# Two scans of a delta rule on one core: half-step order against level-by-level order, and decays off the PE

## The chip, the cores and the metric

One core of a Trainium2 chip runs the whole program. The metric is device time in microseconds (us) of one execution, the median of several runs. Engines are named as in the profile: PE is TensorE's matmul, PEld its weight loads, DVE is VectorE, ACT is ScalarE, POOL is GpSimd, SP is SyncE, whose queue issues DMAs.

## The reference, cut to what matters

The kernel is one layer of a model: a mixer with three branches and a mixture of experts. The change lies in one branch, the gated delta rule, which is scanned in chunks of 128 tokens, forward and backward, with 4 heads of width 128. Context and latent tokens together are 18 chunks, so each direction makes 18 steps.

```python
gc = jnp.cumsum(chunks(g), axis=-1)
diff = gc[..., :, None] - gc[..., None, :]
decay = jnp.where(tri, jnp.exp(jnp.where(tri, diff, 0.0)), 0.0)
m = jnp.where(strict, jnp.einsum('nbhik,nbhjk->nbhij', kb, kc) * decay, 0.0)
a_mat = m + jnp.eye(CHUNK, dtype=f32)
sol = lax.linalg.triangular_solve(a_mat, rhs, left_side=True, lower=True, unit_diagonal=True)
qk = jnp.where(tri, jnp.einsum('nbhik,nbhjk->nbhij', qc, kc) * decay, 0.0)

def step(s, inp):
    qg_i, kg_i, u_i, w_i, qk_i, gl_i = inp
    v_new = u_i - jnp.einsum('bhck,bhkv->bhcv', w_i, s)
    o = jnp.einsum('bhck,bhkv->bhcv', qg_i, s) + jnp.einsum('bhij,bhjv->bhiv', qk_i, v_new)
    s = s * gl_i[..., None, None] + jnp.einsum('bhck,bhcv->bhkv', kg_i, v_new)
    return s, o
```

Per chunk and direction the kernel builds the matrix from the key products and the decays, inverts it (1 + m) in levels of doubling block size, and uses the inverse with the carried state.

## The kernel before, in words

The program runs its stages one after the other with a barrier between them: projections and convolution, the mixer's other branches, `delta_rule` (line 1302), `merge`, the output projection, the choice of experts and the experts. Only `delta_rule` and three lines of the stage ahead of it are touched.

`delta_rule` holds both directions d = 0 and 1. A *half* (lines 1510, 1655, 1778) is one chunk of one direction: its inverse runs through levels 1 to 6. A level is a group of TensorE products `first` (line 1553, 128x64 per head, written at line 1545), a copy of its result to SBUF by ScalarE (`partial`, line 1477), a second group `second` (line 1564, 128x96 per head, line 1575), and VectorE's `update` (line 1726): a predicated copy into `um` and, up to level 4, a transposition of `um` into `tm`. At level 6 TensorE turns `um` itself (`turn_u`, line 1578) and ScalarE copies it to `tm` (`turned`, line 1483). Every link waits for the one before it. Level 1 starts from `mn`, which ScalarE copies after TensorE has turned the matrix `mt` (`turn_m`, line 1650; `matrix`, line 1471).

In the gaps of this chain the half carries other work, in an order written out by hand. From the half before it, the *old* one (the other direction): `values`, `from_state`, `from_chunk` and `state` (lines 1583 to 1614). For the *new* one that comes next (the other direction again): `keys`, `scores`, `known`, `turn_m` on TensorE (lines 1623 to 1653), the decays, and VectorE's `matrix`, `begin`, `rest` (lines 1736 to 1759). Some groups are split by heads to fit: three heads of `keys` in one gap, the fourth in the next. `halves` (line 1355) walks the halves (0, n), (1, n) through 18 steps; the middle 16 steps are a loop with two steps in its body.

The decays of a chunk come from TensorE: VectorE's `gate` (line 1717) multiplies a triangle of ones by the gates' high and low parts (`gth`, `gtl`), two products of 512 columns (`exponents`, line 1616, its matmuls are lines 1620 and 1621) sum them in PSUM, and ScalarE takes the exponential (line 1463). GpSimd multiplies the triangle by beta (`sb`, line 1435). The decays that scale the keys and queries by row are exponentials written to DRAM in the stage ahead (`eg_d`) and loaded for each chunk by SyncE, broadcast over the partitions, with the four tensors of the chunk.

Each direction has four PSUM banks of its own, A to D. A serves `first`, `known` and `state`; B serves `keys`, `turn_m` and `turn_u`; C serves `second`, `scores` and the output; D serves `exponents` and `values`. GpSimd's queue (`head`, line 1431) makes `ke`, `qg`, `kg`, `qk` and renews `um`. SyncE loads a chunk two steps ahead once the state has been updated (line 1404).

## Time and profile before

| what | us |
|---|---|
| median of 3 runs | 4169.45 (4168.18 to 4175.18) |
| the profiled execution | 4168.63 |
| its span | 4167.1 |
| granted clock over the span | 0.979 of full |
| PE busy over the span | 3970.8 (95%) |

A busy time is the time in which at least one instruction of the engine runs. A group of instructions stands with its count and the mean of one; "idle before" is the time its engine waited just before it, with what released it. Times of a timeline are microseconds from the start of the span. A matmul of float32 operands appears as two records, each with its own weight load, so a group over four heads has eight loads; a transposition has one per head.

### The profile page before, as it was taken

To read this page: it belongs to the slowest core of one execution; us is meant where nothing else is said; L and a number is where in the kernel's file an instruction comes from. 1 tells how busy PE (TensorE), PEld (TensorE's weight loads), DVE (VectorE), ACT (ScalarE), POOL (GpSimd) and SP (SyncE) were. 2 spreads that over 40 slices of the span, in tenths; PEclk is the share of its full clock that TensorE was granted. 3 is DMA by queue.
4 is the path that set the end of the run, shared out by engine and by line. 5 is a ranking of instruction groups with operands and counts; after the bars stand their busy time and mean duration, and the time that the engine had idled before them with its cause. 6 is when DMAs were issued, how large, how long until landed. Compare 5 with 4: busy or idle time off the path is not lost. (4 is left out here: it accounts for less than half of the span.)

```text
span 4167.1 us, 57860 instructions
## 1 busy us (share of the span) xinstructions
PE 3970.8 (95%) x20112; PEld 3065.1 (74%) x20112; DVE 2292.2 (55%) x3037; ACT 1531.4 (37%) x2482; POOL 791.7 (19%) x698
## 2 busy tenths in 40 slices
PE   8999999999989999999999999989589999999998
PEld 3444446456769999998778787878478888888887
DVE  4665500356646666665444534344467776777675
ACT  5333411226632222223333424222144444444443
POOL 2999100011113333332000000000100000000000
PEclk9999999999999999999999999999699999999999
DMA  7445341021132222221534444244257676767773
GB/s 289 125 134 140 93 127 39 11 65 33 25 140 65 79 82 78 76 76 41 200 101 169 144 127 152 88 138 152 110 177 215 209 219 206 220 207 217 211 218 101
DMA packets 240185, 551.99 MB, mean 132 GB/s; under 512 B 38316, under 2 KB 99276, under 8 KB 237516
## 3 DMA queue, kind: packets, MB, share of 16 engines
q1 hardware_dynamic: 207964, 435.45, 33.0%
q0 software_dynamic: 32112, 115.11, 9.4%
q8 instruction: 67, 1.10, 0.1%
q14 instruction: 42, 0.34, 0.0%
HBM read 440.44 MB, written 99.68 MB: 130 GB/s over the span
## 5 line engine op out<-in xcount | busy, mean ns | idle before, releaser
L2767 DVE TENSOR_TENSOR sb_we_low<-sb_we,sb_we_high 128x1024 fp32r<-128x1024 f32 x377 | 458.3, 1222 | 121.6 <-ACT sb_we_high L2717 121.6
L2717 ACT ACTIVATE sb_we_high<-sb_we 128x1024 fp32r<-128x1024 f32 x377 | 392.2, 1048 | 142.3 <-PE ey L2681 142.3
L329 PE MATMUL p_ps<-sb_hT,sb_ring 128*128 128x512 f32 (+1 forms) x960 | 373.4, 550 | 1.8 <-ACT sb_raw L462 1.8
L2121 DVE TENSOR_TENSOR sb_wm_low<-sb_wm,sb_wm_high 128x1024 fp32r<-128x1024 f32 x127 | 155.3, 1223 | 399.4 <-ACT sb_wm_high L2034 399.4
L2666 PE MATMUL eg<-sb_xe_parts,sb_we_high 128*128 128x512 f32 x1024 | 373.3, 398 | 1.6 <-DVE sb_xe_parts L2762 1.6
L2666 PE MATMUL eu<-sb_xe_parts,sb_we_high 128*128 128x512 f32 x1024 | 371.9, 396 | 0.0
L329 PEld LDWEIGHTS p_ps<-sb_hT,sb_ring 128*128 128x128 f32 x960 | 181.8, 190 | 188.4 <-issue 180.9
L1976 PE MATMUL pg<-sb_hb_high,sb_wm_high 128*128 128x512 f32 x768 | 304.5, 396 | 9.4 <-DVEq L2093 5.3
L1977 PE MATMUL pg<-sb_hb_low,sb_wm_high 128*128 128x512 f32 x768 | 301.0, 392 | 0.0
L1978 PE MATMUL pg<-sb_hb_high,sb_wm_low 128*128 128x512 f32 x768 | 300.8, 392 | 0.0
L2665 PE MATMUL eg<-sb_xe_parts,sb_we_low 128*128 128x256 f32 x896 | 251.3, 280 | 0.0
L2665 PE MATMUL eu<-sb_xe_parts,sb_we_low 128*128 128x256 f32 x896 | 251.2, 280 | 0.0
L851 PE MATMUL mix_ps<-sb_hT,sb_ring 128*128 128x512 f32 (+1 forms) x544 | 231.7, 583 | 2.7 <-ACTq L1037 2.7
L2625 POOL DMA_INDIRECT out<-sb_ybe,sb_ti x32 | 51.0, 1593 | 889.0 <-DVE sb_ybe L2802 830.5
L2666 PEld LDWEIGHTS eg<-sb_xe_parts,sb_we_high 128*128 128x128 f32 x1024 | 192.5, 188 | 37.0 <-issue 1.8
L2666 PEld LDWEIGHTS eu<-sb_xe_parts,sb_we_high 128*128 128x128 f32 x1024 | 192.4, 188 | 34.5
L2060 ACT ACTIVATE sb_sg<-pg 128x512 f32<-128x512 f32 x96 | 57.1, 595 | 411.3 <-PE pg L1978 411.3
L851 PEld LDWEIGHTS mix_ps<-sb_hT,sb_ring 128*128 128x128 f32 x544 | 103.7, 191 | 126.0 <-issue 125.1
L1976 PEld LDWEIGHTS pg<-sb_hb_high,sb_wm_high 128*128 128x128 f32 x768 | 145.7, 190 | 42.4 <-DVEq L2092 5.5
L2775 DVE TENSOR_REDUCE sb_sue<-eu 128x256 f32<-128x512 f32 x128 | 88.5, 691 | 153.8 <-PE eu L2666 153.8
L2665 PEld LDWEIGHTS eu<-sb_xe_parts,sb_we_low 128*128 128x128 f32 x896 | 168.2, 188 | 6.1
L2665 PEld LDWEIGHTS eg<-sb_xe_parts,sb_we_low 128*128 128x128 f32 x896 | 168.2, 188 | 6.0
(433 smaller groups left out, 8469.0 us busy)
## 6 DMA issues: line engine op xcount, KB each, us to landing
sb_we<-in_w_ex SPq DMA_DIRECT2D x384, 512.0 KB, 4.5
sb_wm<-in_w_gates SPq DMA_DIRECT2D x96, 512.0 KB, 3.6
sb_wrow<-in_w_mod_row POOLq DMA_DIRECT2D x64, 256.0 KB, 3.7
sb_wm<-in_w_br SPq DMA_DIRECT2D x32, 512.0 KB
sb_ring<-in_w_ch POOLq DMA_DIRECT2D x19, 512.0 KB, 4.7
sb_eg<-eg_d SPq DMA_DIRECT2D x36, 256.0 KB, 3.8
sb_lk<-k_d SPq DMA_DIRECT2D x36, 256.0 KB, 4.3
sb_lq<-q_d SPq DMA_DIRECT2D x36, 256.0 KB, 4.6
```

The source lines that it names most:

```text
L329: last = nc.tensor.matmul(ps[:, b % BANKS, 0:wd], w[:, kind, k], g.hT[:, k, t0:t0 + wd], start=(k == 0), stop=(k == KD - 1))
L851: last = nc.tensor.matmul(ps[:, b, 0:wd], w[:, (n + ZF) % 3, k], g.hT[:, k, t0:t0 + wd], start=(k == 0), stop=(k == KD - 1))
L1976: nc.tensor.matmul(bank[:], high, rh[:, k], start=(k == ks[0]), stop=False)
L1977: nc.tensor.matmul(bank[:], high, rl[:, k], start=False, stop=False)
L1978: last = nc.tensor.matmul(bank[:], low, rh[:, k], start=False, stop=(k == ks[-1]))
L2060: a(sg[:, br], pg[br][:], ACT.Sigmoid).then_inc(s.sig, 1)
L2121: v.tensor_tensor(wl[n], w[n], wh[n], ALU.subtract).then_inc(s.wl, 1)
L2665: nc.tensor.matmul(bank[:, 0:CAP], low, xh[:, u, k], start=False, stop=False)
L2666: last = nc.tensor.matmul(bank[:], high, both, start=(k == 0), stop=(k == KD - 1))
L2717: nc.scalar.activation(wh[:, n % CUT], w[:, n % RAW], ACT.Copy).then_inc(s.wh, 1)
L2767: v.tensor_tensor(wl[:, n % CUT], w[:, n % RAW], wh[:, n % CUT], ALU.subtract).then_inc(s.wl, 1)
L2775: v.tensor_reduce(su[:, f % 2], pu[f % 2][:].rearrange("p (a t) -> p t a", a=2), AX_X, ALU.add).then_inc(s.usum, 1)
```

## The change

Both directions of a step now go through the levels together. On every engine a level is direction 0 and then direction 1, and between such pairs stand whole groups of other work: the last step's values, outputs and state, and the next step's set-up. `walk` takes the place of `halves`. The new order of each engine follows (lines of the new code, `both(n, lev)` being the level's copy or update for d = 0, then 1):

```python
def walk(eng, step):
    for n in range(2):
        step(n, n, n > 0, True)
    with eng.Fori(1, STEPS // 2 - 1) as i:
        for u in range(2):
            step(2 * i + u, u, True, True)
    for n in range(STEPS - 2, STEPS):
        step(n, n % 2, True, n < STEPS - 1)
...
# SyncE
def step(n, u, old, new):
    for d in range(2):
        if old:
            store(d, n - 1, place(nc.sync, d, n - 1), 1 - u)
        if not isinstance(n, int) or n < STEPS - 2:
            ahead = place(nc.sync, d, n + 2)
            sem = (s[d].ld0, s[d].ld1)[u]
            sp.wait_ge(s[d].qg, n + 1)
            first_loads(d, ahead, u)
            sp.wait_ge(s[d].kg, n + 1)
            sp.dma_start(lkt[d][u][:], g.kt_d[ahead]).then_inc(sem, 16)
            sp.wait_ge(s[d].r, n + 1)
            sp.dma_start(lvt[d][u][:], g.vt_d[ahead]).then_inc(sem, 16)
...
# GpSimd
def scale(d, n, u):
    q = s[d]
    at = place(nc.gpsimd, d, n)
    pool.wait_ge(q.eg, n + 1)
    wait(pool, q.ks, n)
    tt(ke[d][:], lk[d][u][:], gr[d][u][:], ALU.mult).then_inc(q.ke, 1)
    wait(pool, q.sup, n - 1)
    hold(pool, q.held)
    copy(el[d][u][:], gr[d][u][:, :, last_token(d):last_token(d) + 1]).then_inc(q.el, 1)
    wait(pool, q.op, n)
    tt(qg[d][:], lq[d][u][:], gr[d][u][:], ALU.mult).then_inc(q.qg, 1)
    wait(pool, q.su, n)
    tt(kg[d][:], lkt[d][u][:], col(g.esb, d, at), ALU.mult).then_inc(q.kg, 1)
def scores(d, n, u):
    q = s[d]
    pool.wait_ge(q.qkr, n + 1)
    pool.wait_ge(q.dq, n + 1)
    tt(qk[d][u][:], qr[d][:], dq[d][:], ALU.mult).then_inc(q.qkv, 1)
def step(n, u, old, new):
    for d in range(2):
        if old:
            renew(d, n - 1, 1 - u)
        scale(d, n, u)
        if new:
            scores(d, n + 1, 1 - u)
...
# ScalarE
def row_decays(d, n, u):
    act.wait_ge(s[d].df, n + 1)
    a(gr[d][u][:], gr[d][u][:], ACT.Exp).then_inc(s[d].eg, 1)
def step(n, u, old, new):
    v = 1 - u
    both(n, 1)
    if old:
        values(0, n - 1, v)
    both(n, 2)
    if old:
        output(0, n - 1, v)
    if new:
        row_decays(0, n + 1, v)
        exponent(0, n + 1, v)
    both(n, 3)
    if old:
        values(1, n - 1, v)
    both(n, 4)
    if new:
        raw_scores(0, n + 1, v)
        matrix(0, n + 1, v)
    both(n, 5)
    if old:
        output(1, n - 1, v)
    if new:
        row_decays(1, n + 1, v)
        exponent(1, n + 1, v)
    for d in range(2):
        partial(d, n, 6)
        turned(d, n, u)
    if new:
        raw_scores(1, n + 1, v)
        matrix(1, n + 1, v)
    if isinstance(n, int) and n >= STEPS - 2:
        for i in range(2):
            split_high(2 * (n - STEPS + 2) + i)
...
# TensorE
def turn_u(d, n, u):
    q = s[d]
    pe.wait_ge(q.vu, NL * n + NL - 1)
    if d == 0:
        wait(pe, s[1].vn, n)
    else:
        pe.wait_ge(s[0].t5e, n + 1)
    turn(b_val, um[d][u]).then_inc(q.t5, 1)
def values(d, n, u):
    q = s[d]
    pe.wait_ge(q.vu, NL * n + NL)
    pe.wait_ge(q.r, n + 1)
    pe.wait_ge(s[1].t5e if d == 0 else s[0].vn, n + 1)
    each(b_val, um[d][u], rb[d]).then_inc(q.vp, 1)
def state(d, n, u):
    q = s[d]
    pe.wait_ge(q.kg, n + 1)
    wait(pe, s[1 - d].r, n + 1 + d)
    each(b_state, kg[d], vn[d]).then_inc(q.su, 1)
def known(d, n, u):
    q = s[d]
    pe.wait_ge(q.ke, n + 1)
    pe.wait_ge(q.z, 1)
    wait(pe, q.sup, n)
    wait(pe, s[1 - d].r, n + d)
    each(b_state, ke[d], st[d]).then_inc(q.ks, 1)
def step(n, u, old, new):
    v = 1 - u
    def firsts_of(lev):
        for d in range(2):
            first(d, n, u, lev)
    def seconds_of(lev):
        for d in range(2):
            second(d, n, u, lev)
    firsts_of(1)
    if old:
        values(0, n - 1, v)
    seconds_of(1)
    if old:
        from_state(0, n - 1, v)
    firsts_of(2)
    if old:
        from_chunk(0, n - 1, v)
    seconds_of(2)
    if old:
        state(0, n - 1, v)
    if new:
        keys(0, n + 1, v, (0, 1))
    firsts_of(3)
    if new:
        keys(0, n + 1, v, (2, 3))
    if old:
        values(1, n - 1, v)
    seconds_of(3)
    known(0, n, u)
    firsts_of(4)
    if new:
        scores(0, n + 1, v)
    seconds_of(4)
    if new:
        turn_m(0, n + 1, v)
    if old:
        if new:
            pe.wait_ge(s[0].qkr, n + 2)
        from_state(1, n - 1, v)
    firsts_of(5)
    if old:
        from_chunk(1, n - 1, v)
    seconds_of(5)
    if old:
        state(1, n - 1, v)
    if new:
        keys(1, n + 1, v, (0, 1))
    for d in range(2):
        first(d, n, u, 6)
        turn_u(d, n, u)
    if new:
        keys(1, n + 1, v, (2, 3))
    known(1, n, u)
    seconds_of(6)
    if new:
        scores(1, n + 1, v)
        turn_m(1, n + 1, v)
...
# VectorE
def difference(d, n, u):
    at = place(nc.vector, d, n)
    loaded(dve, d, n, u)
    wait(dve, s[d].dq, n)
    v.tensor_tensor(dec[d][:], gr[d][u][:], col(g.gsums, d, at), ALU.subtract).then_inc(s[d].df, 1)
def clamp(d, n, u):
    dve.wait_ge(s[d].df, n + 1)
    dve.wait_ge(s[d].bar, 1)
    v.tensor_tensor(dec[d][:], dec[d][:], heads(bar[:, d]), ALU.min).then_inc(s[d].cl, 1)
def step(n, u, old, new):
    w = 1 - u
    def both(lev):
        for d in range(2):
            update(d, n, u, lev)
    both(1)
    if new:
        difference(0, n + 1, w)
        clamp(0, n + 1, w)
    both(2)
    if old:
        state(0, n - 1, w)
    both(3)
    if new:
        matrix(0, n + 1, w)
    rest(0, n, u)
    both(4)
    if new:
        begin(0, n + 1, w)
        difference(1, n + 1, w)
        clamp(1, n + 1, w)
    both(5)
    if old:
        state(1, n - 1, w)
    if new:
        matrix(1, n + 1, w)
        begin(1, n + 1, w)
    both(6)
    rest(1, n, u)
    if isinstance(n, int) and n >= STEPS - 2:
        for i in range(2):
            split_low(2 * (n - STEPS + 2) + i)
```

The decays leave TensorE. The stage ahead stores the cumulated gates (`gc_d`) and not their exponentials. SyncE loads them broadcast into `gr`; VectorE subtracts the column of the chunk and takes the minimum with a table `bar` that is 0 in the triangle and -1e30 outside; ScalarE takes the exponential of `dec` in place and, apart from it, of `gr` in place. `gate`, `exponents` and GpSimd's `sb` product are gone; VectorE multiplies by beta's column itself. GpSimd has a small copy more per chunk (`el`, 128x4, the last token's decays). `mn`, `tm` and `qk` have two buffers per direction. The eight PSUM banks are dealt out anew: one `first` and one `second` bank for each direction, and four shared by both (`b_val`, `b_out`, `b_key`, `b_state`), with waits of one direction for the other where they change hands. SyncE's loads two steps ahead are split: cumulated gates, keys and queries once `qg` is made, `lkt` once `kg` is, `lvt` once `rest` is.

```diff
-                        if (n, b) == (NZ, 2):
-                            act.wait_ge(sd.own, 27)
-                            a(g.gdh, gdf, ACT.Copy).then_inc(sd.gh, 1)
...
-                                for j, to in enumerate((g.egc[:, d], g.esb[:, d])):
-                                    a(to, pdec[:, 2 * d + j].rearrange("p (n h) -> p n h", h=H), ACT.Exp).then_inc(sd.ex, 1)
+                                for j, (to, func) in enumerate(((g.gsums[:, d], ACT.Copy), (g.esb[:, d], ACT.Exp))):
+                                    a(to, pdec[:, 2 * d + j].rearrange("p (n h) -> p n h", h=H), func).then_inc(sd.ex, 1)
...
+        lq, lk, lkt, lvt, gr, um, ob, mn, tm, qk = map(four, ("lq", "lk", "lkt", "lvt", "gr", "um", "ob", "mn", "tm", "qk"))
+        el = four("el", 1)
-        bank = [[psum(nc, c, f"dr{d}{b}", (P, H, P)) for b in "abcd"] for d in range(2)]
+        firsts, seconds = ([psum(nc, c, f"dr_{n}{d}", (P, H, P)) for d in range(2)] for n in ("first", "second"))
+        b_val, b_out, b_key, b_state = (psum(nc, c, f"dr_{n}", (P, H, P)) for n in ("val", "out", "key", "state"))
...
-                    act.wait_ge(q.mat, n + 1)
-                    wait(act, q.dq, n)
-                    a(dec[d][:], D_[:], ACT.Exp).then_inc(q.exp, 1)
+                    act.wait_ge(s[d].cl, n + 1)
+                    a(dec[d][:], dec[d][:], ACT.Exp).then_inc(s[d].exp, 1)
...
-                def exponents(d, n, u):
-                    q, (A, B, C_, D_) = s[d], bank[d]
-                    pe.wait_ge(q.gt, 2 * n + 2)
-                    wait(pe, q.vn, n)
-                    mm(flat(D_), after[:, d], flat(gh[d]), start=True, stop=False)
-                    mm(flat(D_), after[:, d], flat(gl[d]), start=False, stop=True).then_inc(q.mat, 1)
...
-                    v.tensor_tensor(dq[d][:], dec[d][:], sb[d][:], ALU.mult).then_inc(q.dq, 1)
+                    v.tensor_tensor(dq[d][:], dec[d][:], col(g.beta, d, at), ALU.mult).then_inc(q.dq, 1)
...
-        g.beta, g.egc, g.esb, g.gdl = (sbuf(nc, c, n, [P, 2, POS, H])[:] for n in ("beta", "egc", "esb", "gdl"))
-        g.gdh = sbuf(nc, c, "gdh", [P, 2, POS, H], F32R)[:]
+        g.beta, g.gsums, g.esb = (sbuf(nc, c, n, [P, 2, POS, H])[:] for n in ("beta", "gsums", "esb"))
```

## Rows read from the trace of the kernel before

**Rows 1.** Busy by stretch: us, then busy us and count of each engine, PEclk, DMA.
```profile
1230.48:1250.80 20.32, 17.00 (x106) 15.29 (x107) 9.23 (x14) 3.55 (x8) 7.43 (x6) 0.83 0.61 228
1499.80:1520.21 20.41, 19.92 (x162) 18.55 (x163) 12.53 (x21) 5.88 (x12) 6.86 (x6) 1.00 0.26 68
1255.00:1935.00 680.00, 662.83 (x5371) 618.38 (x5369) 419.64 (x700) 196.87 (x402) 227.70 (x200) 1.00 0.24 75
```

**Rows 2.** Timeline, where halves start (level 1) and the last values.
```profile
1230.48 1.10 PE L1545 MATMUL dr0a<-sb_um,sb_mn 128*128 128x64 f32 x8 [0.69 <-ACT sb_mn L1475]
...
1253.58 1.08 PE L1545 MATMUL dr1a<-sb_um,sb_mn 128*128 128x64 f32 x8
...
1273.86 1.08 PE L1545 MATMUL dr0a<-sb_um,sb_mn 128*128 128x64 f32 x8
...
1930.63 1.08 PE L1545 MATMUL dr0a<-sb_um,sb_mn 128*128 128x64 f32 x8
...
1971.65 1.16 PE L1545 MATMUL dr1d<-sb_rb,sb_um 128*128 128x128 f32 x8 [0.65 <-DVE sb_um L1730]
```

**Rows 3.** Timeline of one half of direction 1, levels 1 to 5.
```profile
1502.63 0.74 DVE L1730 COPY_PREDICATED sb_um<-sb_consts_sb,dr1c 128x256 f32<-128x256 uint32 x1 [2.35 <-PE dr1c L1575]
...
1503.42 0.97 PEld L1545 LDWEIGHTS dr1a<-sb_um,sb_mn 128*128 128x128 f32 x8 [0.44 <-DVE sb_um L1730]
...
1504.31 0.53 PEld L1596 LDWEIGHTS dr0c<-sb_qg,sb_st 128*128 128x128 f32 x4
...
1504.57 0.38 ACT L1481 ACTIVATE sb_pm<-dr1a 128x256 f32<-128x256 f32 x1 [1.20 <-PE dr1a L1545]
...
1505.00 0.97 PEld L1575 LDWEIGHTS dr1c<-sb_pm,sb_tm 128*128 128x128 f32 x8
...
1505.89 0.75 PEld L1604 LDWEIGHTS dr0c<-sb_qk,sb_vn 128*128 128x128 f32 x6
...
1506.41 0.43 DVE L1730 COPY_PREDICATED sb_um<-sb_consts_sb,dr1c 128x256 f32<-128x256 uint32 x1 [1.35 <-PE dr1c L1575]
...
1506.89 0.97 PEld L1545 LDWEIGHTS dr1a<-sb_um,sb_mn 128*128 128x128 f32 x8 [0.25 <-DVE sb_um L1730]
...
1509.58 0.19 PEld L1620 LDWEIGHTS dr0d<-sb_gth,sb_after 128*128 128x128 f32 x1
...
1510.24 0.97 PEld L1545 LDWEIGHTS dr1a<-sb_um,sb_mn 128*128 128x128 f32 x8 [0.36 <-DVE sb_um L1730]
...
1514.21 1.08 DVE L1766 SCALAR_TENSOR_TENSOR sb_st<-sb_st,sb_eg,dr0a 128x128 f32<-128x128 f32 x4
```

**Rows 4.** By form, 1215 to 1975 us: count | busy us, mean ns of one.
```profile
L1734 DVE STREAM_TRANSPOSE sb_tm<-sb_um 128x512 f32<-128x512 f32 x144 | 102.4, 711 | 5.0
...
L1730 DVE COPY_PREDICATED sb_um<-sb_consts_sb,dr1c 128x256 f32<-128x256 uint32 x108 | 52.6, 487 | 124.0 <-PE dr1c L1575 124.0
...
L1751 DVE COPY_PREDICATED sb_um<-sb_consts_sb,sb_mt 128x512 f32<-128x512 uint32 x36 | 34.1, 947 | 0.3 <-DVE sb_mt L1744 0.2
...
L1741 DVE TENSOR_TENSOR sb_dq<-sb_dec,sb_sb 128x512 f32<-128x512 f32 x36 | 24.9, 692 | 4.0 <-POOL sb_sb L1435 2.2
...
L1499 ACT ACTIVATE sb_ob<-dr0c 128x512 f32<-128x512 f32 x18 | 10.8, 597 | 35.1 <-PE dr0c L1604 35.1
```

**Rows 5.** Line 1720, the gates: duration ns min/median/max.
```profile
L1720 DVE TENSOR_TENSOR sb_gth<-sb_consts_sb,sb_gdh x36: 1010/1019/1515, 1216.1 to 1934.9; 128x512 fp32r<-128x512 f32 x36
L1720 DVE TENSOR_TENSOR sb_gtl<-sb_consts_sb,sb_gdl x36: 651/1350/1360, 1217.1 to 1938.2; 128x512 fp32r<-128x512 f32 x36
```

**Rows 6.** Line 1438, GpSimd: duration ns min/median/max.
```profile
L1438 POOL TENSOR_TENSOR sb_ke<-sb_lk,sb_eg x36: 1265/1713/1722, 1224.3 to 1935.3; 128x512 f32<-128x512 f32 x36
```

**Rows 7.** DMAs of one step (1500 to 1541 us): count, KB, us to landing.
```profile
sb_lvt<-vt_d SPq DMA_DIRECT2D x2, 256.0 KB, 5.5
```

**Rows 8.** Timeline of the start of the stage and of its end.
```profile
1224.28 1.78 PEld L1545 LDWEIGHTS dr0b<-sb_lk 128*128 128x128 f32 x8 [5.44 <-DMA sb_lvt<-vt_d]
...
1974.70 0.60 ACT L1499 ACTIVATE sb_ob<-dr1c 128x512 f32<-128x512 f32 x1 [1.25 <-PE dr1c L1604]
```

More of the change, by code:

```diff
@@ L1539, in _ @@
+                walk(nc.scalar, step)
+                for d in range(2):
+                    values(d, STEPS - 1, 1)
+                    output(d, STEPS - 1, 1)
             @block.tensor
@@ L1655, in half @@
-                def half(cur, old, new):
-                    d, n, u = cur
-                    first(d, n, u, 1)
+                    turn(b_key, mt[d]).then_inc(q.t0, 1)
+                def step(n, u, old, new):
+                    v = 1 - u
+                    def firsts_of(lev):
+                        for d in range(2):
+                            first(d, n, u, lev)
+                    def seconds_of(lev):
+                        for d in range(2):
+                            second(d, n, u, lev)
+                    firsts_of(1)
@@ L1686, in half @@
[L1686 removed]
+                        keys(1, n + 1, v, (0, 1))
+                    for d in range(2):
+                        first(d, n, u, 6)
+                        turn_u(d, n, u)
                     if new:
[L1688 to L1689 removed]
+                        keys(1, n + 1, v, (2, 3))
+                    known(1, n, u)
+                    seconds_of(6)
                     if new:
[L1691 removed]
@@ L1692, in half @@
-                    turn_u(d, n, u)
-                    first(d, n, u, 6)
-                    if new:
-                        turn_m(*new)
-                        known(*new, (2, 3))
-                    second(d, n, u, 6)
-                every = range(H)
-                for d in range(2):
-                    pe.wait_ge(s[d].aft, 1)
-                exponents(0, 0, 0)
-                keys(0, 0, 0, every)
-                known(0, 0, 0, every)
-                scores(0, 0, 0, every)
-                turn_m(0, 0, 0)
@@ L1707, in _ @@
-                halves(nc.tensor, half)
-                end = (1, STEPS - 1, 1)
-                values(*end, every)
-                from_state(*end, every)
-                from_chunk(*end, every)
+                        scores(1, n + 1, v)
+                        turn_m(1, n + 1, v)
+                for d in range(2):
+                    keys(d, 0, 0)
+                    scores(d, 0, 0)
+                    turn_m(d, 0, 0)
+                walk(nc.tensor, step)
+                for d in range(2):
+                    if d == 1:
+                        pe.wait_ge(s[0].oe, STEPS)
+                    values(d, STEPS - 1, 1)
+                    from_state(d, STEPS - 1, 1)
+                    from_chunk(d, STEPS - 1, 1)
@@ L1792, in half @@
-                    update(d, n, u, 5)
+                        state(1, n - 1, w)
                     if new:
-                        begin(*new)
-                        rest(*new)
-                    update(d, n, u, 6)
-                    if turn_of(d, n) is not None:
-                        split_low(turn_of(d, n))
-                for d in range(2):
-                    v.tensor_copy(after[:, d], g.dirt(d, 1)).then_inc(s[d].aft, 1)
-                for part in range(2):
-                    gate(part, 0, 0, 0)
@@ L1803, in _ @@
-                matrix(0, 0, 0)
-                begin(0, 0, 0)
-                rest(0, 0, 0)
-                halves(nc.vector, half)
+                        matrix(1, n + 1, w)
[3 more added lines that the diff above has]
+                    if isinstance(n, int) and n >= STEPS - 2:
+                        for i in range(2):
+                            split_low(2 * (n - STEPS + 2) + i)
+                for d in range(2):
+                    v.tensor_scalar(bar[:, d], g.dirt(d, 0), -1.0, -NEG, ALU.add, ALU.mult).then_inc(s[d].bar, 1)
@@ L1809, in late_data @@
+                for d in range(2):
+                    difference(d, 0, 0)
+                    clamp(d, 0, 0)
+                    matrix(d, 0, 0)
+                    begin(d, 0, 0)
+                walk(nc.vector, step)
 def late_data(t, lev):
```

322 lines of the change are left out of this document (125 added, 197 removed).

## Prediction

> **What bounds the kernel now.** I first look for the stage in the page, then at the busy times by stretch. In the delta rule VectorE works 62% of the time, ScalarE 29%, GpSimd 33%, and PE 97%, at the full clock [rows 1]. A busy time counts pipelined tails, though, so I go to where halves start: 1273.86 for step 1 and 1930.63 for step 17, hence 656.8 us for 16 steps, **41.05 us a step**, 20.5 a half [rows 2]. Then the timeline of one half. A group of eight records starts a slot of its own every 0.89 us: `second` at 1505.00, the next group at 1505.89; `first` at 1503.42, the next at 1504.31 [rows 3]. That is **0.111 us for each weight load**, whatever the width (64, 96 or 128 columns). A half has 160 such loads: 96 of the levels, 56 of seven groups of other work, 8 of two transpositions. That makes 17.8 us. The rest, 2.7 us of a half, is the two `exponents` products (from 1509.58, before the next group at 1510.24, part of which is a wait) and gaps: the level's chain is longer than the work laid into it, as at 1506.89, where PE had waited for VectorE since 1506.56 (1505.89 plus six loads) [rows 3]. So PE's instruction stream is the floor, and a latency chain that is a little too long lies on top of it.
>
> **The chain's lengths.** From the start of `first` to where `second` may start: 1503.42 to 1504.95, when the copy ends, plus 0.05: 1.6 us, of which 0.89 is `first` itself. From the start of `second` to where the next `first` may start: 1505.00 to 1506.89, 1.9 us; 2.1 at level 1, whose predicated copy takes 0.74 instead of 0.43 [rows 3].
>
> **PE in the new order.** A step has 2 × 160 = 320 loads, 35.6 us. I wrote the slots out one after the other from the start of a step (t = 0), 0.89 for a group of four heads and 0.45 for a transposition or two heads, and asked of each group whether what it waits for is there. `first` of d = 0 runs from 0, of d = 1 from 0.89, `values` from 1.78, `second` from 2.67 and 3.56, `from_state` 4.45, level 2 from 5.34, and so on: level 3 from 11.13, level 4 from 16.92, level 5 from 22.7, level 6 from 28.5, the last `turn_m` from 35.2.
> - first to second: the other direction's `first` (0.89) already covers the missing 0.7. No gap in any level.
> - second to first, d = 0: the other `second` and one group, 1.78, cover the missing 1.0 (1.2 at level 1).
> - second to first, d = 1: VectorE is the link. Its copy for d = 1 stands behind copy and transposition of d = 0 (0.49 and 0.71 [rows 4]). At level 1: 3.95 to 4.69, 5.44, then 5.48 to 6.22; `first` is due at 6.23. That is a gap of 0.05. At levels 2 to 4 there is 1 us to spare.
> - VectorE's work between: `difference` and `clamp` of d = 0 from 7.0 to 8.4, before level 2's copy at 9.3; `state` (1.08 [rows 3]) 11.8 to 12.9; `matrix` and `rest` 18.0 to 20.2, before 20.9; `begin` (0.95 + 0.71 [rows 4]), `difference` and `clamp` of d = 1 from 23.3 to 26.7, after which level 5's copy, ready at 26.7, ends at 27.2 for a `first` due at 28.5.
> - step to step: `scores` of d = 1 end at 35.4, ScalarE copies them until 36.05 and only then `mn` until 36.7 (0.60 each [rows 4]). `first` of d = 1 is due 0.89 after the step's start at 35.6, that is 36.5: a gap of 0.2.
>
> **What is removed.** The `exponents` leave PE (about 0.45 us a half once their wait is taken off, 0.66 with it), `gate` leaves VectorE (1.0 and 1.35 us a half [rows 5]), the `sb` product GpSimd. **What is added.** `difference` and `clamp` on VectorE. No row shows them; the nearest of the same kind and size is the product at 0.69 [rows 4], the gates at 1.35 are the upper end [rows 5]. I take 0.7, as they meet GpSimd in few places, and keep 1.35 for the range. A second exponential on ScalarE, 0.60 each, at 8.9 and 26.3, where ScalarE is idle; without that cover it would cost 1.2 a step. A 128x4 copy on GpSimd, between nothing and the 0.6 of ScalarE's 512 columns, in idle time either way. The split loads: direction 0's last is issued at about 20.7 and lands 5.5 later [rows 7]; `difference` wants it at 42.6. Direction 1's is issued at 36.6 and wanted at 60. SyncE's queue waits longer for each, but its stores have two buffers, so nothing is late.
>
> **Two engines at one port.** The gates took 0.65 us once and 1.35 in the median [rows 5], and GpSimd's product 1.27 at least and 1.71 in the median [rows 6]: operations with two inputs in SBUF stretch each other when the two engines' meet. In the new order `begin` and `clamp` of d = 1 meet GpSimd's `ke` and `qg`. With the 0.7 that rows 5 show on top of each, the two end at 28.1 instead of 26.7 and level 5's copy at 28.6, a gap of 0.1, which I add. The Trainium skill (SBUF — State Buffer, "SBUF: two separate sides") says more: a VectorE operation with two SBUF inputs and a GpSimd operation exclude each other, and the later one waits for the whole of the other. Rows 5 and 6 neither refuse that nor need it. The rival that it gives is the second below.
>
> **The sum.** A step: 35.6 + 0.05 + 0.2 + 0.1 = 35.95. The loop's turn and odds: the averaged half is 0.11 over the one of rows 1, so 0.2 a step, kept. **36.2 us**.
> - Steps 1 to 16: 16 × (41.05 − 36.2) = −77.6.
> - Step 0: 43.4 before [rows 2], with a clock of 0.83 in its first half [rows 1]. Now 256 loads (no old work), 28.5, with gaps of 0.7 at two levels without filling and 4.3 for the slow clock: 33.5, −9.9. The old first half took 23.1 for 128 loads [rows 2], 2.6 more than a full one, though it had 3.6 us less to do; its chain's gaps are the rest.
> - Step 17: 41.0 before. Now 280 loads, 31.2, and 1.3 because four of ScalarE's copies for the next stage (0.60 each by rows 4, 2.4, of which `first` and `values` cover 1.1) stand ahead of its first level: −8.5.
> - Start: the first load is there at 1224.28 [rows 8], the first level began 6.2 later [rows 2]. Now both directions must be set up: `difference` 0.7, `clamp` 0.7, exponential 0.65, two products 1.45, `begin` 1.75, then for d = 1 0.7 + 0.7 + 0.65 + 1.45 + 0.7 for `turn_m`: 9.5. +3.3.
> - End: 1971.65 to 1975.30 before, one direction's values and output [rows 2, 8]. Now two, of which the second waits for the first's output in the shared bank: 7.5. +3.9.
> - The stage ahead (one copy and one subtraction of 160 columns fewer): 0.
>
> Sum −88.8 against the profiled 4168.63 (its span is 4167.1): 4079.8. The median of the runs is 0.8 above the profiled one: **4081 us**.
>
> **The rivals.**
> 1. *The gaps return in part.* 90 us rest on every group being ready on time in a stream without slack of its own. One late group moves all behind it. For it: level 1 has no slack and level 5 1.3 us, and 12 cross-direction waits on shared banks are new. Against it: all other slacks are above 0.7. If half of the old gaps stay, 38.1 a step: 17 × 1.9 = 32 more, 4113.
> 2. *Exclusion at the port decides.* If `begin` and `clamp` of d = 1 each wait for a whole product of GpSimd (1.27 [rows 6]), level 5's copy ends at 29.7, a gap of 1.2 where the sum has 0.1: 16 × 1.1 = 18 more, 4099. Rows 5 and 6 show the stretching; against it stands that the gates are gone, so that there are fewer meetings in all. It is what the skill's rule would do here.
> 3. *Slower: VectorE's queue order takes over.* In every level d = 1's copy stands behind d = 0's copy and transposition, and set-up stands ahead of the next level. It decides once each of the six levels loses 0.93 us (5.6 a step, 4.85 of it to break even, the rest for start and end). If each level loses one further copy and transposition (1.2), a step is 43.4 and the kernel about 4215. Against it: VectorE has some 24 us of work in 36, and the slots above leave it 1 us at most levels.
> 4. *The new order brings nothing, only the products' departure does*: the chain of a level stays what PE waits for, 2 × 0.6 a step: 4145.
>
> **The numbers.** Forecast 0.60 (own range 4072 to 4094), rivals 1 and 2 together 0.29, rival 4 0.05, rival 3 0.04, and 0.02 for no difference. A measurement can tell 0.2%, 8 us. The range runs from 4070 (no gap at all, 35.6 a step, less a us or two at the start) to 4122 (rival 1 with the upper price of the new operations). Faster 0.93, same 0.03, slower 0.04.
>
> **What would show it.** Right: `first` of step 17 about 579 us after step 1's; PE's gaps within a step under 1 us; nothing on lines of the products with `after`; the first level of the stage at about 1234. `difference` near 0.7 for d = 0 and above for d = 1. Wrong: PE's weight loads waiting for VectorE's `um` in several levels (rivals 1 and 3), VectorE busy over 27 us a step or its two-input operations at 1.3 (rival 2), or slots longer than 0.111, which would move everything.

## Result and the profile after

The changed kernel took **4075.68 us** (median of 4 runs, 4068.34 to 4079.47) against 4169.1 for the kernel before beside it (4 runs, 4168.18 to 4175.18): ratio **0.9771, interval 0.9754 to 0.9788**. The forecast was 4081, range 4070 to 4122. The profiled execution is the slowest of the four, 4079.47 with a span of 4077.9, so sums below are made against 4079.47 − 4168.63 = −89.2.

First the stage by stretches (columns: us, then busy us and count of PE, PEld, DVE, ACT, POOL, then PEclk, DMA share, GB/s): the first 20 us after both directions' set-up, one whole step, and steps 1 to 16 with their edges. They answer to [rows 1].

```profile
1235.00:1255.00 20.00, 20.00 (x124) 20.00 (x122) 9.91 (x17) 4.42 (x10) 4.84 (x5) 0.66 0.58 215
1522.20:1558.00 35.80, 35.80 (x323) 35.72 (x321) 22.74 (x43) 12.53 (x27) 12.04 (x12) 1.00 0.27 88
1255.00:1845.00 590.00, 588.78 (x5262) 587.23 (x5262) 375.74 (x692) 207.12 (x430) 197.68 (x197) 1.00 0.27 84
```

A step has some 320 weight loads in 35.80 us, and PE is busy for all of it. In 590 us PE stands still for 1.2. VectorE's share is 22.74 us of a step, 64%.

Then PE's timeline, at the places that carry the sum (start and length in us, engine, line, operation, tiles, count; in brackets the idle time ahead and what ended it). They answer to [rows 2] and [rows 8]; lines 1583, 1612 and 1588 of this kernel are the plain products, `second` and the transpositions.

```profile
1225.09 2.07 PE L1583 MATMUL dr_key<-sb_lk 128*128 128x128 f32 x8 [13.30 <-DMA sb_lvt<-vt_d]
...
1234.68 0.66 PE L1588 MATMUL dr_key<-sb_consts_sb,sb_mt 128*128 128x128 f32 x4 [2.56 <-DVE sb_mt L1788]
1235.17 3.32 PE L1583 MATMUL dr_first<-sb_um,sb_mn 128*128 128x64 f32 x16
1238.29 3.67 PE L1612 MATMUL dr_second<-sb_pm,sb_tm 128*128 128x96 f32 x16
...
1264.47 1.10 PE L1583 MATMUL dr_first<-sb_um,sb_mn 128*128 128x64 f32 x8 [1.22 <-DVE sb_um L1774]
...
1271.72 2.01 PE L1583 MATMUL dr_first<-sb_um,sb_mn 128*128 128x64 f32 x16
...
1844.63 2.01 PE L1583 MATMUL dr_first<-sb_um,sb_mn 128*128 128x64 f32 x16
...
1876.55 1.08 PE L1583 MATMUL dr_val<-sb_rb,sb_um 128*128 128x128 f32 x8
...
1880.16 1.16 PE L1583 MATMUL dr_val<-sb_rb,sb_um 128*128 128x128 f32 x8 [0.69 <-ACT sb_ob L1517]
...
1883.20 0.60 ACT L1517 ACTIVATE sb_ob<-dr_out 128x512 f32<-128x512 f32 x1 [1.25 <-PE dr_out L1642]
```

Step 1 starts at 1271.72 and step 17 at 1844.63: 572.9 us for 16 steps, **35.81 a step** where it was 41.05. The weight-load stream inside a step shows why there is next to nothing left to gain from order. From start to start, a group of 8 loads takes 0.89 us and one of 16 takes 1.79, one behind the other; only the first group of a step takes 1.90:

```profile
1522.26 1.98 PEld L1583 LDWEIGHTS dr_first<-sb_um,sb_mn 128*128 128x128 f32 x16
1524.16 0.97 PEld L1583 LDWEIGHTS dr_val<-sb_rb,sb_um 128*128 128x128 f32 x8
1525.05 1.87 PEld L1612 LDWEIGHTS dr_second<-sb_pm,sb_tm 128*128 128x128 f32 x16
1526.84 0.97 PEld L1635 LDWEIGHTS dr_out<-sb_qg,sb_st 128*128 128x128 f32 x8
1527.73 1.87 PEld L1583 LDWEIGHTS dr_first<-sb_um,sb_mn 128*128 128x128 f32 x16
```

Last, groups by form over the whole stage (after the count: busy us and mean ns, then the idle time ahead and its releaser): the new operations and PE's largest groups.

```profile
L1583 PE MATMUL dr_first<-sb_um,sb_mn 128*128 128x64 f32 x1728 | 211.9, 274 | 1.2 <-DVE sb_um L1774 1.2
L1774 DVE COPY_PREDICATED sb_um<-sb_consts_sb,dr_second 128x256 f32<-128x256 uint32 x216 | 102.7, 476 | 188.3 <-PE dr_second L1612 188.0
L1765 DVE TENSOR_TENSOR sb_dec<-sb_dec,sb_bar 128x512 f32<-128x512 f32 x36 | 26.6, 739 | 1.2
L1759 DVE TENSOR_TENSOR sb_dec<-sb_gr,sb_gsums 128x512 f32<-128x512 f32 x36 | 23.8, 660 | 8.0 <-DMA sb_lvt<-vt_d 8.0
L1450 POOL TENSOR_TENSOR sb_qg<-sb_lq,sb_gr 128x512 f32<-128x512 f32 x36 | 53.6, 1488 | 86.9 <-PE dr_out L1642 86.9
L1448 POOL COPY sb_el<-sb_gr 128x4 f32<-128x4 f32 x36 | 14.4, 399 | 0.0
```

`first` waits for VectorE's `um` 1.2 us in the whole stage, while VectorE waits 188 us for PE: the roles are those of a kernel bound by PE's stream.

### The profile page after: what moved, and what is told of

It is laid out like the page before. It is cut to its first block and busy times, and to the rows that moved or that the text cites. A ratio compares the mean times of both kernels' runs of the same rounds, so it can differ in the third digit from the quotient of the medians.

```text
span 4077.9 us, 57895 instructions
## 1 busy us (share of the span) xinstructions
PE 3900.2 (96%) x20032; PEld 3041.6 (75%) x20032; DVE 2249.7 (55%) x3032; ACT 1545.3 (38%) x2517; POOL 764.3 (19%) x697
## 3 DMA queue, kind: packets, MB, share of 16 engines
q1 hardware_dynamic: 207964, 435.45, 33.5%
## 5 line engine op out<-in xcount | busy, mean ns | idle before, releaser
L1583 PE MATMUL dr_first<-sb_um,sb_mn 128*128 128x64 f32 x1728 | 211.9, 274 | 1.2 <-DVE sb_um L1774 1.2
L1612 PE MATMUL dr_second<-sb_pm,sb_tm 128*128 128x96 f32 x1728 | 211.4, 276 | 0.3 <-ACT sb_pm L1499 0.3
L1583 PEld LDWEIGHTS dr_first<-sb_um,sb_mn 128*128 128x128 f32 x1728 | 207.3, 194 | 2.0 <-DVE sb_um L1774 1.4
L1774 DVE COPY_PREDICATED sb_um<-sb_consts_sb,dr_second 128x256 f32<-128x256 uint32 x216 | 102.7, 476 | 188.3 <-PE dr_second L1612 188.0
L1612 PEld LDWEIGHTS dr_second<-sb_pm,sb_tm 128*128 128x128 f32 x1728 | 205.0, 195 | 0.5 <-ACT sb_pm L1499 0.5
```

Source lines behind the costliest of these rows:

```text
L1583: last = mm(out[:, h], lhs[:, h], rhs[:, h], start=True, stop=True)
L1612: last = mm(wide(seconds[d])[:, h], tm[d][u][:, h], pm[d][:, h * HALF:h * HALF + WIDE], start=True, stop=True)
```

## The experiments

The theory: the old order left PE waiting for each level's chain (PE, ScalarE, PE, VectorE), and joining the directions level by level fills these waits until only 320 loads of 0.111 us are left. The rivals: that the departure of the `exponents` products and the gates brought the gain, or that a shorter VectorE did. Ratios are to the kernel before, measured beside it. "Step" is the mean of steps 1 to 16, taken between starts of the same group 16 steps apart. "Stage" is the delta rule's own time: from the end of PE's last product of the stage ahead to the end of the last output copy. It is taken from there because the stage ahead ended anywhere from 1208.2 to 1211.9 us, and at 1211.8 and 1209.4 in two profiled executions of the changed kernel itself, so that the bare end of the delta rule carries up to 3.7 us that are not its own. Step and stage come from one profiled execution of each kernel; the kernel before has 41.05 and 764.3, the changed kernel 35.81 and 672.0.

| kernel | median us (range) | ratio [interval] | step us | stage us |
|---|---|---|---|---|
| decays alone, old order | 4175.06 (4170.04–4178.16) | 1.0003 [0.9993, 1.0013] | 40.95 | 772.0 |
| new, without chunk's part | 4064.39 (4060.34–4068.68) | 0.9739 [0.9723, 0.9755] | 34.02 | 636.9 |
| old, without chunk's part | 4180.29 (4174.35–4187.14) | 1.0019 [1.0009, 1.0028] | 41.43 | 779.0 |
| new, clamp twice | 4080.71 (4077.83–4082.30) | 0.9776 [0.9760, 0.9792] | 35.81 | 677.5 |
| new, 8 more loads a step | 4086.83 (4083.39–4093.17) | 0.9794 [0.9778, 0.9811] | 36.70 | 687.9 |
| new, warm start | 4074.09 (4069.55–4076.28) | 0.9761 [0.9745, 0.9777] | 35.81 | 669.4 |
| new, split loads | 4068.74 (4066.76–4070.41) | 0.9752 [0.9736, 0.9769] | 35.81 | 664.3 |
| new, both | 4068.02 (4066.61–4073.64) | 0.9752 [0.9736, 0.9768] | 35.81 | 666.3 |
| new again | 4078.78 (4067.68–4081.54) | 0.9768 [0.9755, 0.9781] | 35.81 | 672.0 |
| split loads again | 4067.11 (4066.18–4074.49) | 0.9752 [0.9738, 0.9765] | 35.81 | 664.3 |
| split, short warm-up | 4079.90 (4075.03–4085.19) | 0.9776 [0.9763, 0.9789] | 35.81 | 666.3 |
| the same, end in free banks | 4079.01 (4076.11–4081.67) | 0.9772 [0.9758, 0.9785] | 35.81 | 663.1 |

The kernel before took 4173.55 beside rows 1 to 4 of the table, 4171.85 beside rows 5 to 8 and 4173.24 beside rows 9 to 12. The ratio of the changed kernel was 0.9771.

**The decays alone.** The old order, with the products and gates gone:

```diff
-                    mm(flat(D_), after[:, d], flat(gh[d]), start=True, stop=False)
-                    mm(flat(D_), after[:, d], flat(gl[d]), start=False, stop=True).then_inc(q.mat, 1)
...
-                    a(dec[d][:], D_[:], ACT.Exp).then_inc(q.exp, 1)
+                    act.wait_ge(s[d].cl, n + 1)
+                    a(dec[d][:], dec[d][:], ACT.Exp).then_inc(s[d].exp, 1)
```

> The order of the kernel before (half by half), with only the decays moved: no gates, no products of the decays on the PE, no beta product on GpSimd; VectorE subtracts and clamps, ScalarE has a second exponential. Theory A (the gain of the change is the order: in the old order the PE waits at the ends of the levels' chain, and the group behind the products waited for VectorE's um until 1510.19 anyway): 4150 to 4169 us, no more than 20 us of the 93. Rival B (the gain is the work taken off the PE and VectorE, 0.66 and some 1.0 us a half): 24 us or more, 4145 or below.

The time did not move, so that not even a part of the 20 us allowed for came, and a step went from 41.05 to 40.95. Two views of this kernel say why: the windows (1260 to 1830; the second row is the kernel before), and PE's groups by line in the same stretch.

```profile
1260.00:1830.00 570.00, 546.55 (x4453) 513.66 (x4452) 317.28 (x585) 172.92 (x361) 151.14 (x140) 1.00 0.24 75
...
1260.00:1830.00 570.00, 555.67 (x4498) 518.22 (x4497) 350.40 (x585) 163.62 (x334) 188.84 (x165) 1.00 0.25 77
```

```profile
L1542 PE MATMUL dr1a<-sb_um,sb_mn 128*128 128x64 f32 x672 | 91.0, 278 | 9.0 <-DVE sb_um L1723 8.9
L1542 PE MATMUL dr0a<-sb_um,sb_mn 128*128 128x64 f32 x664 | 90.0, 278 | 8.9 <-DVE sb_um L1723 8.9
```

VectorE lost 33 us of work against the kernel before (317.28 for 350.40 in the same window), and PE 9 (546.55 for 555.67), and both became idle time: `first` still waits for VectorE's `um`. 4452 loads of 0.111 are 494 us, so PE's stream stands for 76 us of 570, 5.5 us a step. The engines' work was not what the old order was short of.

**The chunk's part of the output left out, in both orders.** These two kernels leave the product of `vn` and `qk` out of the output: 16 loads a step, and no other engine's work.

```diff
-                    for h in every:
-                        last = mm(b_out[:, h], vn[d][:, h], qk[d][u][:, h], start=False, stop=(h == H - 1))
```

> The new kernel without the eight loads per direction and step of from_chunk (the part of the output that comes from the chunk itself is left out). Theory A (the PE's stream of loads, 0.111 us each, is the bound in the new order): 16 loads x 0.111 x 18 steps = 32 us below the new kernel, 4044. Rival C (the chain through VectorE and ScalarE is still the bound of the new order): under 10 us below it.

> The kernel before without the same group. Theory A: its loads lie in gaps whose ends ScalarE and VectorE set (level 2 to 3), so the PE only waits longer: 0 to 5 us below 4169. Rival C (both orders are bound by the same thing): the same saving as in the new order.

The new order went from 35.81 to 34.02, −1.79, which is 16 × 0.112, and its delta rule took 35.1 us less where 32 were expected. The old one went from 41.05 to 41.43: it did not win. Of the 0.38 that it lost, 0.2 is one step of 44.6 us in which the clock fell (0.88 from 1330 to 1358); most others take 41.2 to 41.35 where they took 41.0 to 41.2 before. Its time came out above the 0 to 5 us less that were expected, and 6.4 us of that in its profile are step 17, which took 47.4 us, with a clock of 0.73 from 1960 to 1975.

PE's weight loads show the chain, in this kernel and then in the kernel before, at the same levels of a half of direction 0:

```profile
1527.15 0.97 PEld L1545 LDWEIGHTS dr0a<-sb_um,sb_mn 128*128 128x128 f32 x8 [0.43 <-DVE sb_um L1728]
...
1530.56 0.97 PEld L1545 LDWEIGHTS dr0a<-sb_um,sb_mn 128*128 128x128 f32 x8 [0.80 <-DVE sb_um L1728]
...
1533.98 0.97 PEld L1545 LDWEIGHTS dr0a<-sb_um,sb_mn 128*128 128x128 f32 x8 [0.36 <-DVE sb_um L1728]
```

```profile
1523.91 0.97 PEld L1545 LDWEIGHTS dr0a<-sb_um,sb_mn 128*128 128x128 f32 x8 [0.43 <-DVE sb_um L1730]
...
1527.32 0.97 PEld L1545 LDWEIGHTS dr0a<-sb_um,sb_mn 128*128 128x128 f32 x8
...
1530.74 0.97 PEld L1545 LDWEIGHTS dr0a<-sb_um,sb_mn 128*128 128x128 f32 x8 [0.36 <-DVE sb_um L1730]
```

From level to level it takes 3.41 and 3.42 us in both, though less lies between in the first. A whole step has twelve such intervals, from 2.8 us (level 6 to the next half) to 3.8. In the step from 1523.4 eleven of them are within 0.01 us of those of the kernel before (the step from 1520.2); the twelfth, between levels 2 and 3 of direction 1, grew from 3.35 to 3.52. So the step of the old order hangs on its chain, and not on how many loads PE has in it. In the new order a level of both directions takes 35.81 / 6 = 5.97 on average, less than 2 × 3.41.

The new order's median is only 11 us below the changed kernel's, which taken alone would suit rival C. The rest went elsewhere: the profiled execution was 17 us shorter (span 4060.5 for 4077.9), of which the delta rule gave 35.1 and the stage ahead 3.0, but from the experts' first product to the end it took 1136.2 instead of 1115.0. There PE waits for nothing that the profile names; the chain of waits by line, this kernel's:

```profile
PEld eg L2720 <- issue: 17.8, 12, 3.1
```

(17.8 us in 12 waits, the longest 3.1; the changed kernel has 2.0 in one on the like line.) The delta rule's own time, not the kernel's, is therefore the measure in this experiment.

**The clamp twice.** Some 1.4 us more of VectorE's work in a step (2 × 0.7):

```diff
+                    v.tensor_tensor(dec[d][:], dec[d][:], heads(bar[:, d]), ALU.min).then_inc(s[d].cl, 1)
+                    dve.wait_ge(s[d].cl, 2 * n + 1)
```

> The new kernel with the clamp of VectorE done twice (0.69 us more per direction and step on VectorE and on the way to the exponential). Theory A (VectorE has slack at every level): 0 to 4 us above the new kernel. Rival C (VectorE's queue is the next bound): 18 x 1.38 = 25 us above it.

```profile
1260.00:1830.00 570.00, 568.05 (x5076) 566.56 (x5076) 391.91 (x698) 201.09 (x413) 195.16 (x191) 1.00 0.28 86
```

VectorE was busy for 391.91 us, 31 more than the 360.93 of the changed kernel in this window, where 32 clamps of 0.69 would be 22, since about every other one of the second clamps takes 1.65 us. A step still took 35.81: VectorE binds nothing in a full step. The delta rule as a whole took 5.5 us longer, all of it at its start. The set-up ahead of the first level, which nothing covers, grew by 1.5, and step 0 by 4.0: PE's wait for `um` at level 6 was 1.95 instead of 1.22, and the clock was still at its lower level in 1245 to 1255, where the changed kernel's was back at the higher one from 1249. The median is 5 us above the changed kernel's, the ratio 0.9776 for 0.9771.

**Eight more loads.** Two heads of `first` once more at level 3, for each direction (four products and so eight weight loads a step), into free columns of the bank:

```diff
+                    if lev == 3:
+                        each(spare(firsts[d]), mn[d][u], late(um[d][u][:], d, lev), range(2))
```

> The new kernel with two products more (four weight loads, about what the two products of the decays took: 0.45 us) per direction and step on the PE, into columns of PSUM that nobody reads, ahead of level 3's first group. Theory A (every load counts in the new order): 36 x 0.445 = 16 us above the new kernel, so that moving the decays is worth some 16 us there although it may be worth less in the old order. Rival C: under 5 us, hidden in waits.

A step took 36.70, +0.89, 8 loads of 0.111, and the delta rule 15.9 us more, as expected; the median is 11 us above the changed one's, the ratio 0.9794 for 0.9771. Together the three experiments bracket the new order: taking loads away or adding them moves a step by 0.111 us each, and adding to VectorE by nothing.

**The start of the stage.** The changed kernel's first 64 loads of levels ran at 0.21 us each (3.32 us for 16, above). Two ways were tried: products of a constant ahead of the first keys and between the directions' set-ups, to keep PE at work (`warm(34)`, `warm(8)`), and first loads of both directions issued ahead of the later ones, on semaphores of their own, so that the set-up can begin sooner.

```diff
+                warm(34)
...
+                    if d == 1:
+                        warm(8)
```

```diff
-    LOADS = 5 * 16
+    LOADS, LATER = 3 * 16, 2 * 16
...
+                for d in range(2):
+                    first_loads(d, pos(d, 0), 0)
+                for d in range(2):
+                    later_loads(d, pos(d, 0), 0)
```

> The new kernel with 42 products of the identity ahead of the first keys (34, while the first loads are under way) and ahead of the second direction's first transposition (8). The trace of the new kernel shows the PE at the lower clock level (groups of 16 loads take 3.3 instead of 1.8 us) until about 1249, after a wait for the loads of 13 us. If that wait is what lowers the clock: step 0 5 to 7 us shorter, the kernel 4 to 7 us faster than the new one. If not: unchanged, or up to 2 us slower.

> The new kernel with a semaphore of its own for gates, keys and queries, whose first loads go ahead of the values' of both directions: the first product no longer waits for the chunk's fifth load. Expected: the first keys 2 to 3 us earlier than 1225.1, the kernel 2 to 3 us faster, nothing in the steps. Rival: the transfers share the rings, all land together, no change.

> Both of the last two edits, with 26 instead of 34 products ahead of the first keys: if they add, 7 to 10 us below the new kernel.

Set-up is the time from the end of the stage ahead to the first level, step 0 the time from there to the first level of step 1, all from profiled executions:

| kernel | set-up us | step 0 us |
|---|---|---|
| changed kernel; again | 23.4; 23.4 | 36.55; 36.54 |
| warm start | 24.9 | 32.45 |
| split loads; again | 21.4; 21.3 | 30.87; 30.87 |
| both | 21.9 | 32.35 |
| split, short warm-up | 21.8 | 32.46 |
| the same, end in free banks | 21.2 | 30.88 |

The warm products made step 0 4.1 us shorter, less than the 5 to 7 expected, and the set-up 1.5 longer: 2.6 us in the stage, and a ratio (0.9761) that cannot be told from the changed kernel's. The split loads made the set-up 2.0 shorter (1.3 of it the earlier first keys, for which 2 to 3 had been expected), and step 0 5.7 shorter, which was not expected: its clock was at the higher level. Both together didn't add: the stage gained 5.7 us, 2.0 less than with the split alone, as the keys were held up until 1224.9, where the 26 products ended, and the clock fell again for a while in step 0 (0.79 from 1257 to 1261). The changed kernel and the split were measured again beside one another:

> The new kernel as it is, beside the versions that start it differently, on one chip. 4068 to 4080, median near 4076; the width should come from the PE's clock in the stage's first 30 us, so that the span of an execution and its mean clock go together.

> The separate load semaphores again. If the 7 us of the first look are real, about 4069 with a width of 4 us; of it 3 to 4 us are the earlier first load and the rest the clock, which in that profile was at its higher level from 1226 on instead of falling at 1235. If the clock was luck, 3 to 4 us below the new kernel.

The changed kernel came out as expected, and in its five executions (as in the four of the result) the shortest, 4067.68, has the highest mean clock (0.979) and the two longest, 4078.90 and 4081.54, the lowest (0.975 and 0.976). That the clock is lost in the stage's first 30 us, only the profiled ones show. So the same kernel varies by 14 us, and its mean clock with it, the repeated split by 8. First PE's timeline of the repeated changed kernel, then that of the repeated split and a window of it:

```profile
1222.70 2.08 PE L1583 MATMUL dr_key<-sb_lk 128*128 128x128 f32 x8 [13.29 <-DMA sb_lvt<-vt_d]
...
1232.28 0.66 PE L1588 MATMUL dr_key<-sb_consts_sb,sb_mt 128*128 128x128 f32 x4 [2.56 <-DVE sb_mt L1788]
1232.77 3.27 PE L1583 MATMUL dr_first<-sb_um,sb_mn 128*128 128x64 f32 x16
```

```profile
1220.69 2.08 PE L1591 MATMUL dr_key<-sb_lk 128*128 128x128 f32 x8 [11.92 <-DMA sb_lq<-q_d]
...
1229.61 0.66 PE L1596 MATMUL dr_key<-sb_consts_sb,sb_mt 128*128 128x128 f32 x4 [1.44 <-DVE sb_mt L1796]
1230.10 1.96 PE L1591 MATMUL dr_first<-sb_um,sb_mn 128*128 128x64 f32 x16
```

```profile
1225.00:1245.00 20.00, 17.47 (x149) 16.65 (x148) 14.62 (x24) 7.25 (x15) 6.57 (x6) 0.99 0.96 354
```

The keys are there 2.0 us sooner than beside it (1220.69 for 1222.70; 0.6 of that is the stage ahead), the first level starts 2.7 sooner (1230.10 for 1232.77), and it runs at the full clock of 2.4 GHz, where the changed kernel had 0.50 in 1235 to 1245. Step 0 is 5.7 shorter. So of the 8.3 us by which the stage ends sooner (1873.1 for 1881.4), 5.7 are step 0 at the higher clock, 2.0 the shorter set-up and 0.6 not the delta rule's. The medians lie 11.7 us apart and both measurements of the split agree (4068.74, 4067.11), though the intervals of the two ratios (0.9738 to 0.9765, 0.9755 to 0.9781) overlap. With the split and warm products together, whose median is the same, it is the best version, some 106 us below the kernel before.

> Separate load semaphores and 12 products of the identity ahead of the first keys (26 ran on until 1224.9, past the loads' landing at 1221.3, and held the keys up by 3.6 us). Expected: first keys at 1221.3, clock at its higher level in the stage's first steps: 0 to 3 us below the separate loads alone.

> The one before, with the last values and output of direction 1 in banks that are free by then, so that they no longer wait for direction 0's output: the stage's end from the last second group's end to the last output 7.25 us in the new kernel, about 6.2 here. 1 us faster than the one before, which the medians can hardly show; the trace can.

The first of these two adds `warm(12)` to the split loads. The second also gives direction 1's last values and output banks of their own:

```diff
-                    if d == 1:
-                        pe.wait_ge(s[0].oe, STEPS)
-                    values(d, STEPS - 1, 1)
+                    values(d, STEPS - 1, 1, (b_val, b_key)[d])
```

The end fell from 7.25 to 6.19 us (1868.69 to 1874.88), as expected, as the bank's wait of 0.69 and its neighbours are gone. But both kernels came out 12 to 13 us above the split loads alone, where 0 to 3 below had been expected. Little of that is in their delta rule, which took 2.0 us more in the first and 1.2 less in the second (1.1 of it at the end) than with the split loads. From the experts' first product to the end they took 1121.8 and 1126.6 where the split kernel has 1113.6, with waits of PE that name no releaser. The second kernel's:

```profile
PEld eg L2736 <- issue: 6.8, 7, 2.0
PEld eg L2735 <- issue: 6.7, 6, 1.7
```

So the gain at the end is real in its stage and was not seen in the whole. What makes these waits is open: three kernels have them, and another with nearly the same cut (the old order without the chunk's part) doesn't.

## Why the prediction was right

The forecast case came true: 4075.7 for 4081, and in the profile −89.2 for −88.8. The mechanism was right: PE's load stream is the floor of the new order, and the chain that lay on top of it is covered. That the sum agrees within 0.4 us is luck in part, since errors of −7 and +7 us cancel, and since the profiled execution is the slowest of four. The terms, measured in it:

| term | forecast | measured |
|---|---|---|
| stage ahead | 0 | +0.8 |
| start | +3.3 (to 9.5) | +3.9 (10.1) |
| step 0 | −9.9 (33.5) | −6.8 (36.6) |
| steps 1 to 16 | −77.6 (step 36.2) | −83.9 (step 35.81) |
| step 17 | −8.5 (32.5) | −9.1 (31.9) |
| end | +3.9 (7.5) | +3.6 (7.25) |
| stages behind | 0 | +2.3 |
| sum | −88.8 | −89.2 |

- **The floor was read rightly**: 320 loads at 0.111 are 35.6 of the 35.81. The runs with loads taken away and added confirm both the price and that nothing else binds.
- **The additions to it were too many**: 0.55 for gaps, port and loop's turn, of which 0.2 came, so 6.2 us more were gained in 16 steps. Of that, 0.12 stands in the first group of a step, which takes 1.90 us for 1.79 (1522.26 to 1524.16) and for which 0.2 had been forecast. The gaps of 0.05 at level 1 and of 0.1 for the port stand nowhere in the step's stream of loads.
- **Step 0 was priced 3.1 too low.** The slow clock was taken at 4.3 us. The first four groups of 16 loads took from 1235.17 to 1248.58, 13.4 us where 7.1 are due, 6.3 for the clock alone; the other 1.8 of 36.6 − 28.5 are gaps, where 0.7 had been put, and 1.22 of it is the wait at 1264.47. The prediction's 4.3 goes with the clock of 0.83 that the kernel before had there, and the changed kernel's stretch has 0.66. This term is also the one that changes from execution to execution (with split loads step 0 was 30.87).
- **The start** was forecast for "about 1234" and came at 1235.17. 0.8 of the 1.2 lies in the stage ahead, whose last product on PE ended at 1211.8 for 1211.0; in other executions that point moves by as much as 3.7 us.
- **`difference` and `clamp`**: 0.66 and 0.74 in the mean, for 0.7. The GpSimd copy takes 0.40, inside the bounds of 0 and 0.6, in idle time.
- **Stages behind**, taken at no change, took 2.3 longer. 1.0 of it comes before the experts: the merge's first products, of 512 columns, take 0.63 us or more each until 1893.8 (clock 0.50), twelve of them, while in the kernel before the seventh already took 0.60 and the tenth 0.39. The other 1.4 lie from the experts' first product on and were not traced.
- **The prices of rivals 3 and 4** don't quite follow from the terms given with them: 18 × 7.2 us makes 4211 and not 4215, 18 × 1.2 makes 4148 and not 4145. Nothing hangs on it.

**Rival 1** (gaps return, 38.1 a step) fell: 35.81. **Rival 3** (VectorE's order takes over, slower) fell: PE waited 1.2 us for `um` in the stage, and even 31 us more of VectorE's work cost a step nothing. **Rival 4** (only the products' departure helps) was tested by itself and is the wrong way round: their departure alone brought nothing, 1.0003, and all of the gain needs the order. The order without the departure was not run; by the 0.111 of a load or the 0.45 of the two products a half, it would be about 0.9 us a step worse than the changed kernel, an estimate.

**Rival 2** (exclusion at the port) had its mechanism right, but its price was not met in a step, and the gap that was to follow from it did not come. The timeline of the changed kernel where the engines meet, and where they don't:

```profile
1508.99 1.27 POOL L1445 TENSOR_TENSOR sb_ke<-sb_lk,sb_gr 128x512 f32<-128x512 f32 x1
1509.72 1.13 DVE L1795 COPY_PREDICATED sb_um<-sb_consts_sb,sb_mt 128x512 f32<-128x512 uint32 x1
...
1512.20 0.69 DVE L1765 TENSOR_TENSOR sb_dec<-sb_dec,sb_bar 128x512 f32<-128x512 f32 x1
1512.34 1.69 POOL L1450 TENSOR_TENSOR sb_qg<-sb_lq,sb_gr 128x512 f32<-128x512 f32 x1 [1.48 <-PE dr_out L1642]
...
1519.50 0.73 DVE L1795 COPY_PREDICATED sb_um<-sb_consts_sb,sb_mt 128x512 f32<-128x512 uint32 x1 [0.17 <-DVE sb_mt L1788]
1530.77 1.27 POOL L1450 TENSOR_TENSOR sb_qg<-sb_lq,sb_gr 128x512 f32<-128x512 f32 x1 [3.30 <-PE dr_out L1642]
```

The operation that comes second is longer, 1.13 for 0.73 and 1.69 for 1.27, and the first keeps its time, 1.27 and 0.69. The second is delayed by 0.40 and 0.42, where the two overlap by 0.54 and 0.55, and not by a whole product of GpSimd, because the other had already run in part. What the Trainium skill says (SBUF — State Buffer, "SBUF: two separate sides"), that the two exclude each other instead of sharing the bandwidth, agrees with these rows as far as the first keeps its time; the delay is a little short of the overlap. No level came late, and the kernel with two clamps shows that a larger delay would not have mattered either. There one meeting in each step costs the second clamp 0.96 us, nearly what the rival had put, and the step is still 35.81:

```profile
1729.28 0.69 DVE L1765 TENSOR_TENSOR sb_dec<-sb_dec,sb_bar 128x512 f32<-128x512 f32 x1
1729.40 1.70 POOL L1450 TENSOR_TENSOR sb_qg<-sb_lq,sb_gr 128x512 f32<-128x512 f32 x1 [1.47 <-PE dr_out L1642]
1730.01 1.65 DVE L1767 TENSOR_TENSOR sb_dec<-sb_dec,sb_bar 128x512 f32<-128x512 f32 x1
```

## What to carry to other kernels

When an engine looks 97% busy, take the start-to-start time of its instructions and multiply by their count: here that gave 35.6 of 41.05 and named the 5.4 us that the busy share hid. Most of it was waiting: with the two products of the decays gone as well, PE still waited 5.5 us a step. If a dependent chain of several engines sets a loop's time (its period stays, 3.4 us here, whatever is taken from between), lighter engines bring nothing and a second, independent chain laced into it brings nearly all. Once the stream is full, look at the ends, at the first loads and at the clock there.

## What was not expected of the hardware

- **The clock at the start of a stage is a term of its own.** The decays-alone kernel has the order of the kernel before, but PE stood idle for 13.3 us ahead of its first keys, where in the kernel before the products of the decays split this wait into 7.4 and 4.7 us. In 1225 to 1275 it had a granted clock of 0.67 where the kernel before had 0.89, and from its first level to its first `values` it took 31.4 us instead of 24.0; with this and a set-up 1.9 longer, its delta rule was 7.7 us longer in the profile although 16 steps had won 1.6. The rows of the decays-alone kernel and of the kernel before:

```profile
1225.00:1275.00 50.00, 45.54 (x266) 42.97 (x265) 21.25 (x36) 10.03 (x22) 12.48 (x11) 0.67 0.31 114
...
1225.00:1275.00 50.00, 45.57 (x329) 42.19 (x328) 27.08 (x42) 11.68 (x25) 17.09 (x15) 0.89 0.44 160
```

- **What goes with it, but isn't shown to cause it.** In six of the fourteen profiled executions PE had stood idle for 13.1 to 13.4 us ahead of the first keys, and all six ran their first levels at the lower level, 1.2 GHz, in whole or for the most part (the changed kernel in most of 1235 to 1249). In the other eight, with shorter waits (11.9 us with split loads, less in the rest), the first level ran at 2.4 GHz. No experiment changed the wait alone: the split loads also shortened PE's next wait, for `mt`, from 2.56 to 1.44 us.
- **Keeping PE at work with products of a constant isn't a sure cure**: four kernels with them reached the full clock at their first level, but in three the clock fell again around 1257 to 1266 (to 0.57 in 1262 to 1266 with the warm start), and these gained less in the stage than the one that only loads sooner. The fourth gained no more than that one, apart from its shorter end.
- **Waits without a releaser far behind the edit.** Three kernels that differ from others only in the delta rule lost 8 to 21 us in the experts' stage, over 1000 us behind it, with such waits on PE's line of the first gate products. No run tells what they are; a difference under 0.3% between two layouts of a kernel should be read stage by stage before it is put down to the edit.
